# Spreading expert gates on TensorE: two accumulating matmuls of 128 columns a token in place of one of 256

## The reference

```python
def peer_layer(h, w_q, sub_keys, u_emb, v_emb):
    q = (hf @ w_q).reshape(t, PEER_HEADS, 2, PEER_QDIM // 2)
    sc = jnp.einsum('thcd,hcnd->thcn', q, sub_keys)
    sv, si = lax.top_k(sc, PEER_TOPK)
    ...                                    # 16 best pairs a head: expert 128 * i + j
    gates = jax.nn.softmax(fs, axis=-1)
    ue = u_emb[ic]
    act = jax.nn.gelu(jnp.einsum('cd,chkd->chk', xc, ue))
    ve = v_emb[ic]
    return jnp.einsum('chk,chkd->cd', gc * act, ve)
```

## Time and profile before

| | |
|---|---|
| median of 3 runs | 914.39 us (913.66 to 914.93) |
| the profiled execution | 914.13 us, of it 912.4 us from the first to the last instruction |
| PE busy | 900.6 us, 99% of the span |
| PEld busy | 791.3 us, 87% |
| DVE busy | 726.5 us, 80% |
| ACT busy | 559.9 us, 61% |
| POOL busy | 425.5 us, 47% |
| granted TensorE clock | 9 tenths of full speed or more in each of 40 slices, 1.00 in the stretches below |
| gates' groups | from 340 to 549 us of the span |

### The profile page before, as it was taken

One profiled execution on the slowest core, in us unless ns is written; L12 is line 12 of the kernel. 1 busy time (PEld: TensorE's weight loads), 2 busy tenths in 40 slices (PEclk: granted clock), 3 DMA queues, 4 the chain that ended last, 5 costly groups with the idle time before them and its releaser, 6 DMA issues.

```text
span 912.4 us, 19224 instructions
## 1 busy us (share of the span) xinstructions
PE 900.6 (99%) x5348; PEld 791.3 (87%) x5348; DVE 726.5 (80%) x1635; ACT 559.9 (61%) x1126; POOL 425.5 (47%) x340
## 2 busy tenths in 40 slices
PE   7999999999999999999999999999999999999998
PEld 6776889899999999999999999888888888888886
DVE  6889634189999339999999996888888888888886
ACT  6658566655555556666666666565665656656663
POOL 3975278788888887777777774000000000000000
PEclk9999999999999999999999999999999999999999
DMA  9643150466666665565556556777777777777773
GB/s 338 231 159 119 68 208 1 162 218 225 228 229 229 230 229 196 186 219 196 191 188 216 197 184 238 247 235 248 241 240 242 232 245 247 239 243 234 245 246 129
DMA packets 67756, 191.54 MB, mean 210 GB/s; under 512 B 6672, under 2 KB 8592, under 8 KB 67728
## 3 DMA queue, kind: packets, MB, share of 16 engines
q1 hardware_dynamic: 67296, 191.00, 61.8%
q10 hardware_dynamic: 432, 0.19, 0.1%
HBM read 173.86 MB, written 17.30 MB: 210 GB/s over the span
## 4 chain that ended last, share of the span: by engine, by line
PE 93%; DVE 2%; ACT 2%; POOL 1%; issue 1%; DMA 1%; ACTq 0%; POOLq 0%; DVEq 0%
PE ps L435 22%; PE ps L437 22%; PE ps L436 22%; PE ps L740 13%; PE ps L742 6%; PE ps L750 3%; ACT routing L1450 1%; PE ps L739 1%; DMA vec<-in_vecs 1%; POOL w_lo L1723 0%; ACT w_hi L1381 0%; PE ps L713 0%; PE ps L591 0%; DVE ps L813 0%; PE ps L427 0%
## 5 line engine op out<-in xcount | busy, mean ns | idle before, releaser
L1599 ACT ACTIVATE w_hi<-raw 128x512 fp32r<-128x512 f32 x512 | 308.2, 628 | 130.9 <-PE ps L437 129.1
L1738 POOL TENSOR_TENSOR w_lo<-raw,w_hi 128x512 fp32r<-128x512 f32 x256 | 326.9, 1299 | 73.9 <-ACT w_hi L1599 73.6
L813 DVE TENSOR_TENSOR w_lo<-raw,w_hi 128x512 fp32r<-128x512 f32 x256 | 177.2, 692 | 52.5 <-ACT w_hi L1599 41.0
L435 PE MATMUL ps<-w_hi,hot_gate 128*128 128x512 f32 x512 | 199.2, 389 | 0.0
L436 PE MATMUL ps<-w_lo,hot_gate 128*128 128x512 f32 x512 | 199.2, 389 | 0.0
L437 PE MATMUL ps<-w_hi,hot_gate 128*128 128x512 f32 x512 | 199.2, 389 | 0.0
L740 PE MATMUL ps<-h_both,w_hi 128*128 128x512 f32 x504 | 181.7, 397 | 0.6 <-POOL w_lo L1738 0.6
L435 PE MATMUL ps<-h_both,w_hi 128*128 128x256 f32 x584 | 165.6, 284 | 0.0
L437 PE MATMUL ps<-h_both,w_lo 128*128 128x256 f32 x584 | 165.2, 283 | 0.0
L436 PE MATMUL ps<-h_both,w_hi 128*128 128x256 f32 x584 | 165.2, 283 | 0.0
L742 PE MATMUL ps<-h_both,w_lo 128*128 128x256 f32 x441 | 123.8, 281 | 0.0
(11 more groups left out here) (230 smaller groups left out, 1157.2 us busy)
## 6 DMA issues: line engine op xcount, KB each, us to landing
raw<-in_u_t SPq DMA_DIRECT2D x128, 512.0 KB, 3.4
raw<-in_v SPq DMA_DIRECT2D x128, 512.0 KB, 3.3
act_spill<-acts SPq DMA_DIRECT2D x62, 256.0 KB, 2.2
acts<-act_spill SPq DMA_DIRECT2D x62, 256.0 KB, 3.4
routing<-in_w_in SPq DMA_DIRECT2D x4, 2048.0 KB, 11.1
routing<-in_w_out SPq DMA_DIRECT2D x2, 2048.0 KB, 8.3
routing<-in_w_q SPq DMA_DIRECT2D x2, 2048.0 KB, 7.8
routing<-in_w_in SPq DMA_DIRECT2D x2, 1024.0 KB, 10.6
```

Source lines behind the costliest of these rows:

```text
L435: pe.matmul(dst, s_hi, m_hi, start=first and i == 0, stop=False)
L813: return V.tensor_tensor(out_, a, b, op)
L1599: A.activation(w_hi[:, 2 * (s % 2) + h, :], raw[:, s, h * HALF:(h + 1) * HALF], ACT.Copy)\
L1738: G.tensor_tensor(w_lo[:, slot, :], raw[:, s, h * HALF:(h + 1) * HALF], w_hi[:, slot, :].bitcast(F32), ALU.subtract).then_inc(lo_ready, 1)
```

## The change

Each token of a group gets two matmuls of 128 columns in place of one of 256: the high part's, which starts the accumulation, and the low part's, which adds to the same 128 columns of PSUM. Both have the same weights, `hot_j` of the token. The sum of both parts is then in PSUM, a group fills one bank (4 or 5) in place of two, ACT's copy writes the finished table and itself counts `group_done`. DVE's `group_out` goes, with its semaphore. All else stays: the values stage still uses banks 4 to 7.

```diff
                         for q in range(GT):
-                            mm = pe.matmul(ps[:, 4 + 2 * (s % 2) + q // 2, (q % 2) * 2 * NKEY:(q % 2 + 1) * 2 * NKEY],
-                                           hot_j[:, s % 2, q, :], hot_gate[:, s % 2, q].rearrange("p a i -> p (a i)"),
-                                           start=True, stop=True)
+                            for a in range(2):
+                                mm = pe.matmul(ps[:, 4 + s % 2, q * NKEY:(q + 1) * NKEY], hot_j[:, s % 2, q, :],
+                                               hot_gate[:, s % 2, q, a, :], start=(a == 0), stop=(a == 1))
                         mm.then_inc(group_psum, 1)
...
-            def group_out(g, b):
-
-                dve.wait_ge(group_high, g + 1)
-                parts = ps[:, 4 + 2 * b:6 + 2 * b, :].rearrange("p b (t a i) -> p (b t) a i", t=2, a=2)
-                tt(routing[:, bass.ds(g * GT, GT), :], routing[:, bass.ds(g * GT, GT), :], parts[:, :, 1, :],
-                   ALU.add).then_inc(group_done, 1)
-
             def one_hots(t, first=False):
...
-                    if not (first and s == 0):
-                        group_out(g - 1, (s - 1) % 2)
...
-            group_out(S // GT - 1, 1)
             dve.wait_ge(group_done, S // GT)
...
             def group_out(g, b):
 
                 act.wait_ge(group_psum, g + 1)
-                parts = ps[:, 4 + 2 * b:6 + 2 * b, :].rearrange("p b (t a i) -> p (b t) a i", t=2, a=2)
-                A.activation(routing[:, bass.ds(g * GT, GT), :], parts[:, :, 0, :], ACT.Copy).then_inc(group_high, 1)
+                A.activation(routing[:, bass.ds(g * GT, GT), :], ps[:, 4 + b, :].rearrange("p (t i) -> p t i", t=GT),
+                             ACT.Copy).then_inc(group_done, 1)
```

More of the change, by code:

```diff
@@ L276, in build @@
         hot_ready, group_psum = sem("one_hots_ready"), sem("group_in_psum")
-        group_high, group_done = sem("group_high_out"), sem("group_done")
+        group_done = sem("group_done")
         w_steps, w_ready, product_done = sem("weighted_steps"), sem("weighted_ready"), sem("product_done")
```

## The result

| | before | after |
|---|---|---|
| median | 914.05 us (913.66 to 914.93) | 939.99 us (939.63 to 940.16, 4 runs) |
| ratio | | 1.028 (95% interval 1.0267 to 1.0293) |
| the profiled execution | 914.13 us, span 912.4 | 939.63 us, span 937.8 |

The kernel became 2.8% slower. The forecast was 943 us, with 936 to 1004 as its range and 937 to 947 as that of the case taken as the likeliest.

A forecast was written before the change was run, and what follows sets the result against it. PE was taken to bound the kernel, busy throughout the groups' stretch. The profiled 914.1 us plus 29 us for the added matmuls' weight loads, nothing for DVE, ACT or code, gave 943.1, forecast as 943; range 936 to 1004.

The forecast's parts named there:

- the case taken as the likeliest: Groups' narrow matmuls each paced by their own weight load: kernel at 943 us, own range 937 to 947, chance 0.56.
- The bound: Stretch of the groups, 209.2 us: PE busy in all of it, so a microsecond of PE is one of the kernel.
- The load's pitch: Groups' 128-column matmuls: 0.116 us each with own load, so 0.93 us a group for 0.475, 29 us more in all.
- DVE's work costs and gives nothing: Groups' stretch: DVE loses 64 additions of 0.688 us, 44 us of busy time, with nothing gained in kernel time.
- Accumulation at no price: Gates' matmuls: accumulating into the same columns twice in a row costs nothing extra.
- ACT's copy at no price: Group's copy on ACT: still 512 elements a partition, 0.586 us, from one bank in place of two, no cost.
- no cost from the longer loop body: PE's loop body on a turn grows from 88 to 104 matmuls; nothing taken for code.
- Four passes: Narrow float32r gates' matmuls handled like plain F32, two records with a load each: 997 to 1006 us, chance 0.33.
- Columns set the pitch: Groups: eight matmuls of 128 columns take what four of 256 take, +0 to +1 us: 914 to 915, chance 0.05.
- the case in between: Groups: eight matmuls take 0.65 us by the Trainium skill's gap for streams with loads; kernel near 925 us, chance 0.04.

The follow-up runs named there:

- the split alone: Kernel before with each gates' matmul split into two of 128 columns, nothing accumulated, DVE's addition kept: 940.38 us, ratio 1.0277.
- half weights: Changed kernel with gates' matmul weights of 64 columns in place of 128, gates of the upper half of the j left out: 918.36 us, ratio 1.0038.

## Why the prediction was right, point by point

- **The bound.** Right: PE's pitches set the time before and after, and the loss sits in the 64 groups alone.
- **The load's pitch.** Right in kind, somewhat high in size. I took 0.116 us between 0.109 and 0.120; it is 0.112. It is the pitch of the plain F32 rows, not float32r's 0.120 at 256 columns. Of the two rows, the one of 64 columns carries the argument: plain F32 records of 256 columns start 0.216 us apart at L609, so those of 128 columns would come at 0.108 by their columns alone, and their 0.111 says little. In the row of 64 columns I averaged in a short first step of 0.06 us; the other steps are 0.111 to 0.112, and not 0.108. The group costs 0.89 and not 0.93 us: +0.42 in place of +0.453, 64 x 0.42 = 27 us in place of 29.
- **A small term that I didn't have.** Between groups the products got shorter. The stretch grew by 25.5 us to 234.7, not by 27, and I had forecast 238. The wide slots' sixteen matmuls, without the shift behind the group, take about 0.03 us less a slot, 1.5 us in all: the step from L740 to L742 is 0.230 us on average, where it was 0.233. It is there in the split alone, and not when only the addition is gone. But it isn't simply due to eight narrow matmuls in front: with half weights there are eight as well, and the step is 0.236. Why is open.
- **DVE's work costs and gives nothing.** Right, and shown by taking the addition away alone. But its busy time fell by 33 us (726.5 to 693.4), not by 44: records of DVE overlap (the addition's, from 402.22 to 402.91 us, and that of `hot_j` behind it, from 402.82), and 64 times 0.688 us counted each overlap as work. The added durations of all its records fell by 41 us.
- **Accumulation at no price, ACT's copy at no price, no cost from the longer loop body.** Nothing of these is seen. The split alone, which accumulates nothing and adds on DVE, has the same time. The longer loop body is in both of these kernels and has no run of its own, but PE has no idle time in the stretch.
- **Four passes (0.33).** Fell: 512 records, and a pitch of 0.060 us for the narrow float32r matmul once its load is short. The upper half of my range was there for this case alone.
- **Columns set the pitch (0.05), and the case in between (0.04).** Fell. The 0.058 us at L713, which I let speak for the first, is no stream of single loads: its records and loads start in pairs, 7 ns apart within a pair and 0.11 us from pair to pair. Its operands lie on 64 rows, the lower or the upper half in turn. The Trainium skill's 56 and 81 ns at 128 columns ("TensorE: Matmul & The Clock Gate", section "Back-to-back issue gap") are not what float32r with full loads shows: 112 ns. The section "LDWEIGHTS (loading the stationary operand)" of that page gives 107 ns for the load by itself, and that is within 5% of the trace. The 56 ns, which the page gives for a matmul by itself, is near what the runs show where the load is short: 58 to 60 ns with half the weights.

## What to carry to other kernels

In a stream in which each matmul has its own weights, price it as the larger of its own columns' time (0.116 to 0.120 us for 256 float32r columns) and its successor's load (0.112 us for 128 columns of weights over all 128 rows), and not as columns alone. Cutting a moving operand much below 256 columns then buys almost nothing (1.4 us for half the columns of 256 matmuls); splitting one of 256 columns in two costs nearly a load, even where the weights are unchanged, and work taken from an engine that isn't the bound doesn't pay for it. So use up to 256 columns a matmul before adding another, and keep an addition on VectorE as long as VectorE has the time.

## What the runs showed of the hardware that I had not expected

- Only one load runs ahead of the matmul in progress: behind a matmul of 512 columns (0.23 us) just one load of 0.112 us is hidden, and the second starts with the next matmul, at 399.96 us in the timeline above. In the stretch of the groups, before and after the change, no load record starts ahead of the start of the matmul in front of its own. The exceptions of the trace are products on part of the rows or columns, as at L713, whose loads go in pairs.
- The time of a load appears at the wrong place in the records. The first narrow matmul behind a long one shows 0.06 us, and the long one behind the group shows 0.28 in place of 0.23. Only the sum over the group and its neighbour can be compared.
- A load of 64 columns of weights has a duration of 135 ns against 192 for 128 columns, with 0.060 us of pitch or less against 0.112: the duration has a part that overlaps with the next load, and it isn't the price. Nor does it go by columns alone: the loads of L559, plain F32 and 128 columns too, have durations of 138 to 143 ns.
